# Eight experts fed through one DMA list: the down product's weights are asked for by ScalarE in place of SyncE

## The reference, cut to what matters

```
h = xb @ w_in[e]                                   # 1024 -> 2 x 2816
y = (silu(h[:, :D_FF]) * h[:, D_FF:]) @ w_out[e]   # 2816 -> 1024
```

## Time and profile before

| | |
|---|---|
| median of 3 runs | 1971.63 us (1967.21 to 1972.1) |
| the profiled execution | 1966.17 us, its span 1964.4 us |
| mean granted TensorE clock | 0.985 |
| PE busy | 1791.7 us (91% of the span) |
| DVE, ACT, POOL busy | 520.0, 250.9, 159.5 us |
| the 8 experts, from the first up half to the last down half | 534.2 to 1283.5 us of the span |
| issues of 1 MB up loads, 704 KB down loads | 176 and 128, all by SyncE |
| data moved over the whole span | 498 MB, mean 254 GB/s |

### The profile page before, as it was taken

How to read it: one execution, slowest core, us unless ns; L and a number is a source line. 1 busy time by engine, 2 the same in 40 slices (tenths; PEclk the granted TensorE clock), 3 DMA queues, 4 the chain that set the end, 5 groups by cost and what they waited for, 6 DMA issues and landing times.

```text
span 1964.4 us, 52825 instructions
## 1 busy us (share of the span) xinstructions
PE 1791.7 (91%) x24496; PEld 1405.7 (72%) x24496; DVE 520.0 (26%) x1239; ACT 250.9 (13%) x657; POOL 159.5 (8%) x307
## 2 busy tenths in 40 slices
PE   8999999999998989898989999989989999989775
PEld 7759885666588888888888888877757778653331
DVE  2631000233310101010101010137773443242223
ACT  2310000033110000000000000011222112110000
POOL 0000000100018100000000000035530000000000
PEclk9999999999999999999999999989999999999998
DMA  7225343421498988989898989970301018679996
GB/s 317 108 101 180 147 166 112 172 108 44 176 387 324 383 342 364 369 352 378 353 387 351 401 346 398 347 272 23 129 22 66 34 38 359 239 281 426 426 426 282
DMA packets 72155, 498.08 MB, mean 254 GB/s; under 512 B 8120, under 2 KB 16848, under 8 KB 34512
## 3 DMA queue, kind: packets, MB, share of 16 engines
q1 hardware_dynamic: 61888, 490.12, 62.9%
q10 hardware_dynamic: 10128, 5.97, 1.0%
HBM read 494.99 MB, written 1.05 MB: 253 GB/s over the span
## 4 chain that ended last, share of the span: by engine, by line
PE 67%; DMA 25%; DVE 4%; issue 2%; ACT 1%; ACTq 1%; SPq 0%; DVEq 0%
DMA ringbuf<-in_ein 13%; PE pb L1165 12%; PE pb L809 11%; PE pb L818 7%; DMA ringbuf<-in_eout 5%; PE pb L814 5%; PE pb L1197 4%; PE pb L882 3%; PE pb L1067 3%; DMA cst<-in_e2in 2%; PE pb L1409 2%; PE pb L1386 2%; DMA ringbuf<-in_e2in 2%; PE pb L1675 2%; PE pb L1112 2%
## 5 line engine op out<-in xcount | busy, mean ns | idle before, releaser
L1165 PE MATMUL pb<-arena,ringbuf 128*64 128x80 f32 x11264 | 420.0, 234 | 29.8 <-DMA ringbuf<-in_ein 12.6
L1165 PEld LDWEIGHTS pb<-arena,ringbuf 128*64 128x64 f32 x11264 | 401.4, 137 | 48.7 <-issue 34.5
L1197 PE MATMUL pb<-arena,ringbuf 128*64 128x80 f32 x5632 | 213.8, 234 | 31.6 <-DMA ringbuf<-in_eout 29.6
L1197 PEld LDWEIGHTS pb<-arena,ringbuf 128*64 128x64 f32 x5632 | 201.7, 137 | 43.9 <-DMA ringbuf<-in_eout 23.6
L1737 DVE TENSOR_TENSOR arena<-arena,pb 128x160 f32<-128x160 f32 (+3 forms) x130 | 48.0, 369 | 650.9 <-ACT arena L2706 404.6
L809 PE MATMUL pb<-XT,ringbuf 128*128 128x256 f32 (+2 forms) x1104 | 202.6, 346 | 0.8 <-ACT XT L2506 0.8
L809 PEld LDWEIGHTS pb<-XT,ringbuf 128*128 128x128 f32 (+1 forms) x1104 | 181.3, 193 | 21.8 <-issue 2.1
L2506 ACT ACTIVATE arena<-pb 128x256 f32<-128x256 f32 (+5 forms) x188 | 72.6, 404 | 561.0 <-PE pb L1197 203.8
L818 PE MATMUL pb<-arena 64*64 64x64 f32 (+4 forms) x664 | 106.2, 323 | 6.0 <-DVE Y L1737 3.5
L818 PEld LDWEIGHTS pb<-arena 64*64 64x64 f32 (+4 forms) x664 | 51.8, 152 | 57.2 <-issue 29.5
L814 PE MATMUL pb<-ringbuf,arena 128*128 128x512 f32 x192 | 85.1, 602 | 2.9 <-DVE arena L1737 1.8
(11 more groups left out here) (391 smaller groups left out, 1838.5 us busy)
## 6 DMA issues: line engine op xcount, KB each, us to landing
ringbuf<-in_ein SPq DMA_DIRECT2D x176, 1024.0 KB, 7.4
ringbuf<-in_eout SPq DMA_DIRECT2D x128, 704.0 KB, 6.3
arena<-in_e2in SPq DMA_DIRECT2D x13, 2048.0 KB, 26.5
ringbuf<-in_e2in SPq DMA_DIRECT2D x12, 2048.0 KB, 35.3
ringbuf<-in_fin SPq DMA_DIRECT2D x11, 2048.0 KB, 8.0
ringbuf<-in_e2out SPq DMA_DIRECT2D x8, 2048.0 KB, 31.0
ringbuf<-in_wo SPq DMA_DIRECT2D x6, 2048.0 KB, 8.1
arena<-in_e2out SPq DMA_DIRECT2D x6, 2048.0 KB, 33.7
```

The source lines that it names most:

```text
L1165: ins = pe.matmul(PB[4 + f % 2][h_, t * C1:(t + 1) * C1], w3[:, k, (t % 2) * 128 + h_.start:(t % 2) * 128 + h_.stop], XG[e % 2][:, k, :], ...
L1197: ins = pe.matmul(PB[d % 2][h_, 0:C1], w3[:, j, h_], HT[:, f, :], start=f == 0, stop=f == 21)
```

## The change

The down product's loads, from step 2 of expert 0 on, are taken out of SyncE's list and put into ScalarE's program, on ScalarE's own DMA queue. After each copy of an even step `2i`, ScalarE waits for and issues the four loads of steps `2i + 2` and `2i + 3`; after the last even step (`i` = 3) these are steps 0 and 1 of the next expert. SyncE keeps the up product's loads and, for expert 0, steps 0 and 1 of the down product. Slots, sizes, semaphores and the work of all other engines stay.

```
+            def load_out(e, d, x):
+                k = out_slot(d, x)
+                a.wait_ge(*out_free(e, d, x))
+                a.dma_start(OUT1[k], dr["eout"][e, d][:, 1408 * x:1408 * x + 1408]).then_inc(loop_out[k], 16)
+
             def even_dims(e):
                 for i in range(4):
                     a.wait_ge(*dnP.at((1, e, 2 * i, 1)))
                     if e and i % 2 == 0:
                         a.wait_ge(*tuP.at((1, e - 1, i // 2)))
                     copy(YT[:, 2 * i, :], PB[0][:, 0:C1]).then_inc(*A.up(ytA, (e, i)))
+                    for d in (2 * i + 2, 2 * i + 3):
+                        for x in range(2):
+                            if d < 8:
+                                load_out(e, d, x)
+                            elif e + 1 < NE1:
+                                load_out(e + 1, d - 8, x)
...
             for e in range(NE1):
                 for f in range(2 if e == 0 else 0, 11):
                     load_in(e, f)
-                for d in range(2 if e == 0 else 0, 8):
-                    load_out(e, d)
             chunks_to(nu + RING)
```

## The result

The changed kernel takes 1978.27 us (median of 6 runs, 1975.52 to 1980.27) against 1971.01 us for the kernel before in the same series (median of 6, 1967.21 to 1977.36). The ratio is 1.0034 (95% interval 1.0020 to 1.0048): slower by 0.34%, about 7 us. The prediction had 1962. An execution more than 1.5% above the fastest of its kernel is left out of every ratio in this document (three did so: 2602, 4594 and 4594 us).

A forecast was written before the change was run, and what follows sets the result against it. The prediction took the chain of loads as the bound: 94.4 us per expert where TensorE and the DMA engines each could do 83. Its terms, -5.8 - 9.1 + 5.6 = -9.3 us, gave 1962 us from 1971.6, range 1942 to 1985.

The forecast's parts named there:

- (a): Between down and up phases: SyncE asks for early up loads sooner, so the waits of seven up phases go; -5.8 us.
- the hole of the earlier trace: Between up and down phases, 970 to 976 us: DMA engines nearly idle at 14 GB/s, to be filled by early up loads.
- Just behind it: Start of the down phase: first down loads asked for at 9.6 us, as early up loads finish streaming at about 9 us.
- (b): Up phase: the fifth up load lands at 8.1 us, not 10.5, saving 1.3 us per phase; -9.1 us (0 to -16.5).
- (c): Down phase: ScalarE asks late for the first loads of each four; 31.4 us per phase, +5.6 us in all (-8.8 to +33).
- L: Down phase: latency of a pair's first load, taken as 4.8 us between ends of 3.9 and 6.5.
- The chain 21.8 + 2L: Down phase: its predicted length in us from waits, landings and halves, with two latencies of a pair's first load; 31.4 us.
- 0.5 us for roughness: Down phase: allowance in its predicted chain, beside landings 1.73 us apart with no gap within a pair.
- (d): Up phases and last expert: next expert's first four down loads hide under the up phase, `in_u` leaves earlier; costed at nothing.
- The late pair decides: Rival, down phase: a pair's first load takes near 5.9 us, phase 33.6 us; +8 us, 1980 us; chance 0.28.
- Nothing comes of it: Rival, whole kernel: up phases gain nought, and the removed waits are paid for by late down loads; 1972 us; chance 0.15.
- Everything comes: Rival, whole kernel: down phases 29.8 us, up phases gain 2.2 us each; -28 us, 1943 us; chance 0.17.

The follow-up runs named there:

- sp_up_early: Kernel before, one SyncE list, with the next expert's first four up loads moved ahead of the loads of down step 2; ratio to before 1.0025, 1975.8 us.
- sp_same_order: The changed kernel's order of loads, but all issued from SyncE's one list, no load late; ratio to the kernel before 0.9974, 1967.3 us.
- act_steps_2_7: Changed kernel, but down steps 0 and 1 go back to SyncE behind their own expert's last up load; ratio to before 1.0064, 1984.0 us.
- sp_half_early: Kernel before, one SyncE list, with only the next expert's first two up loads moved ahead of down step 2; ratio to before 0.9928, 1958.4 us.
- sp_early_3: Kernel before, one SyncE list, with three of the next expert's up loads moved ahead of down step 2; ratio to before 0.9924, 1958.3 us.
- sp_late_first: Kernel before with one added wait: SyncE asks for an even down step's first half only when both halves are free; ratio 1.0040, 1980.7 us.
- act_on_time: Changed kernel, but ScalarE issues each even step's first-half load ahead of its wait for the second half and the copy; ratio to before 0.9989, 1967.3 us.

## Why the prediction was wrong, point by point

**(a)** The waits went, and by a little more than forecast: -7.0 us for -5.8. But "I put no range on this one" was wrong. The early up loads don't fill the hole of the earlier trace rows for nothing. In expert 0, with 2.5 us between the phases and not 6.5, the first down load stands behind them at 7.4 us and the down phase takes 4.0 us longer (34.8 for 30.8), about 1 us of it at the lowered clock. sp_up_early shows the same in experts 0 to 6, where four down loads go ahead of them. The 9 us of streaming was worked out right. "Just behind it" was the step where a margin should have been asked for.

**(b) is the step that failed.** Forecast -9.1 us, measured +3.1, within what the phases vary among themselves (55.3 to 59.1 us in one execution). The working put the end of the next expert's four down loads at 5.6 us after the start of the up phase, and the fifth up load at 8.1. They ended at 10.9, and it landed at 10.0 to 11.3, where it had landed before. The four down loads simply took the place of the three up loads that had stood ahead of it. What broke is the step "they end at 1.73 us each at about 5.6 us, so the fifth lands at 5.6 + 2.5". It starts from the latency of a lone load and lets the rest land as in a burst. In the trace the first of the four took 6.7 us and not 3.9 (5.0 to 6.7 over the seven experts); one or two of step 7's loads were still in flight when it was asked for (at 1009.21; they landed at 1009.4 and 1011.1). It landed 3.3 us after the start (1.9 to 3.3) and not 0.4, and 3.3 + 3 x 1.73 + 2.51 gives the 11.0 us that were measured. In sp_same_order, where no load is late, the four do end at 5.6 to 6.7 us, and still the fifth up load lands at 8.3 to 11.4: 2.7 to 5.8 us behind the last of them, 3.9 on the mean, and not 2.5. So the step fails in one list too, and the second queue isn't needed for it, though the queues did share the engines: from 1019.0 to 1023.6 SyncE's moved 1.88 MB and ScalarE's the last 0.05 MB of the down load that landed at 1023.6. That loads in flight are what sets the landings apart is argued from these times, not shown. The other half of (b) was right: where only one or two up loads, or none, stand between down step 7 and the fifth up load, and no down load, it lands at 7.2 to 8.9 us, and the up phase takes 55.0 to 55.1 us (sp_up_early, act_steps_2_7, sp_half_early, sp_early_3), which is the 1.3 us per phase that was taken.

**(c)** L was right: 4.64 us over the pairs of steps 4 and 6 of all experts (4.1 to 5.8) for 4.8. The term built on it was not: +1.7 us per down phase and not +0.7, +13.6 in all for +5.6. Of the 13.6, 4.0 are expert 0's and belong to (a). In the other seven the phase grew by 1.4 us. The chain 21.8 + 2L gives 31.1 us with the measured L, and experts 1 to 6 took 32.0. The landings are uneven: a late pair's first load lands 2.1 to 3.9 us behind the load before it (2.9 on the mean), the others 1.6 to 3.2 (1.9), so the 0.5 us for roughness was too little; and about 1 us in one of the six is the lower clock. sp_late_first measures the lateness by itself: +0.40%, 8 us in the timed runs.

**(d)** Right for `in_u`, which left at 1258.38, at the end of the last up phase, and no load is waited for ahead of the first product behind. Its other part, that the four down loads "hide under the up phase", is what (b) fell over.

**The rivals.** *The late pair decides* came nearest in time (1980 us for 1978) but not by its condition: L would have had to be 5.4 us or more and was 4.64. It was the nought in (b) that let a cost of 8 to 9 us decide. *Nothing comes of it* had (b) right, but (c) took more than (a) gave. *Everything comes* was ruled out by (b). The order's gain is real but 5 us of the 14.9. The rule of the Trainium skill (DMA: Bandwidth & Descriptors, section "Issuing engines are not separate DMA queues") that several issuers save just the issue time agrees with act_on_time against sp_same_order (0.15% apart, not to be told from nought); it doesn't speak of the order of one list, which was worth 0.7% here.

**What stays open.** Why landings come 2 to 3 us apart when few loads are in flight, and 1.7 us apart in a burst. How much of each kernel's difference is the lowered clock, since no run holds it fixed. And whether more could be had than the 0.9924 of sp_early_3.

## What to carry to other kernels

When a load is moved forward, write down the next load that somebody waits for and what will be in flight when it is asked for; the gain of a move lasts only as long as nothing urgent stands behind it, and two early loads gave what four took back. An engine that must do something else in order ahead of its issues asks late; half a step of lateness cost 0.4% here, more than its own queue gave. Keep loads of different urgency in one list and in the order of need, unless the second queue never holds an unhurried load while the first has an urgent one.

## What the runs showed of the hardware that had not been expected

- Two queues share the DMA engines without regard to need: a 704 KB load took 8.6 us with a 1 MB load asked for in the same instant on the other engine's queue, and 5.4 us with that load one half later. In the first case both queues moved bytes at once, 0.94 and 0.72 MB in 5 us.
- With few loads in flight the stream has gaps: in the kernel before, the second load of each down phase, asked for 1.5 us behind a lone one, landed 2.7 to 4.1 us after it, though loads asked for back to back land 1.7 us apart.
- A wait can cost more than its length: at or just behind waits for a load of 2.14 and 4.11 us, and of 3.3 us in sp_up_early, TensorE was granted 1.2 GHz, and such down phases had 1 to 2 us more of busy time. Others had no such fall, as behind a wait of 2.01 us in the kernel before.
- The cost of crowding is steep: three early up loads gave 0.9924 and four 1.0025, a cliff of 1% from one load per expert.
